# One-hot rows for eight tokens by three 16-bit VectorE instructions, gate matmuls in groups of sixteen, in an encoder trunk with retrieval layers

## The reference

```python
def peer_ffn(x, norm_g, w_query, sub_keys, u_table, v_table):
    h = rmsnorm(x, norm_g).reshape(T, D)
    q = (h @ w_query).reshape(T, PEER_HEADS, 2, PEER_DHALF)
    s = jnp.einsum('thpd,hpnd->thpn', q, sub_keys)
    vals, idx = lax.top_k(s, 16)
    cand = vals[:, :, 0, :, None] + vals[:, :, 1, None, :]
    cidx = idx[:, :, 0, :, None] * 128 + idx[:, :, 1, None, :]
    top_s, pos = lax.top_k(cand.reshape(T, 8, 256), 16)
    experts = jnp.take_along_axis(cidx.reshape(T, 8, 256), pos, axis=-1)
    gates = jax.nn.softmax(top_s, axis=-1)
    act = gelu(einsum('td,ted->te', h, u_table[experts]))      # 128 experts of 16384 for each token
    return einsum('te,ted->td', gates * act, v_table[experts])
```

## Time and profile before

| | |
|---|---|
| median of 3 runs | 1985.92 us (1985.66 to 1987.83) |
| span of the profiled execution | 1985.3 us, 42726 instructions |
| TensorE matmul busy | 1949.5 us (98%) |
| TensorE weight load busy | 1712.1 us (86%) |
| VectorE busy | 1559.7 us (79%) |
| ScalarE busy | 1313.5 us (66%) |
| mean granted TensorE clock | 0.994 of full speed |
| DMA | 326.15 MB, 164 GB/s over the span |

### The profile page before, as it was taken

How to read it: one execution, slowest core, us unless ns; L and a number is a source line. 1 busy time by engine, 2 the same in 40 slices (tenths; PEclk the granted TensorE clock), 3 DMA queues, 4 the chain that set the end, 5 groups by cost and what they waited for, 6 DMA issues and landing times.

```text
span 1985.3 us, 42726 instructions
## 1 busy us (share of the span) xinstructions
PE 1949.5 (98%) x13762; PEld 1712.1 (86%) x13762; DVE 1559.7 (79%) x3516; ACT 1313.5 (66%) x2799; POOL 17.5 (1%) x21
## 2 busy tenths in 40 slices
PE   8999999999999999999998999999999999999998
PEld 7778999999998777788876699999999977777887
DVE  5455699988889999755578657998888899996555
ACT  5454444589998999644465644445899989995444
POOL 0000000000000000000000000100000000000000
PEclk9999999999999999999999999999999999999999
DMA  6504455544444455555544144555444445545554
GB/s 217 170 12 163 146 182 188 180 162 167 163 165 161 167 169 169 181 188 184 189 172 135 54 160 149 170 184 197 157 160 168 161 163 165 168 169 188 184 188 158
DMA packets 89490, 326.15 MB, mean 164 GB/s; under 512 B 10064, under 2 KB 10192, under 8 KB 89040
## 3 DMA queue, kind: packets, MB, share of 16 engines
q1 hardware_dynamic: 88848, 323.00, 48.7%
q10 hardware_dynamic: 576, 2.33, 0.3%
HBM read 324.24 MB, written 1.05 MB: 164 GB/s over the span
## 4 chain that ended last, share of the span: by engine, by line
PE 93%; DVE 4%; ACT 2%; issue 1%; DMA 0%; DVEq 0%; ACTq 0%
PE ps L1467 37%; PE ps L1259 15%; PE ps L1260 14%; PE ps L1261 14%; PE ps L1418 3%; PE ps L1283 2%; PE ps L1284 2%; PE ps L1285 2%; DVE wl L748 1%; PE ps L1356 1%; PE ps L1399 1%; PE ps L1230 1%; PE ps L1350 0%; PE ps L1519 0%; ACT big L437 0%
## 5 line engine op out<-in xcount | busy, mean ns | idle before, releaser
L748 DVE TENSOR_TENSOR wl<-raw,wh 128x1024 fp32r<-128x1024 f32 x612 | 748.6, 1229 | 190.3 <-ACT wh L419 182.5
L419 ACT ACTIVATE wh<-raw 128x1024 fp32r<-128x1024 f32 x612 | 642.2, 1051 | 230.2 <-PE ps L1261 96.8
L1259 PE MATMUL ps<-hTh,wh 128*128 128x256 f32 x2376 | 684.0, 288 | 2.0 <-DVE hTl L758 2.0
L1260 PE MATMUL ps<-hTl,wh 128*128 128x256 f32 x2376 | 672.4, 283 | 0.0
L1261 PE MATMUL ps<-hTh,wl 128*128 128x256 f32 x2376 | 672.1, 283 | 0.0
L1259 PEld LDWEIGHTS ps<-hTh,wh 128*128 128x128 f32 x2376 | 455.4, 192 | 2.9 <-issue 1.8
L1260 PEld LDWEIGHTS ps<-hTl,wh 128*128 128x128 f32 x2376 | 455.5, 192 | 0.0
L1261 PEld LDWEIGHTS ps<-hTh,wl 128*128 128x128 f32 x2376 | 455.2, 192 | 0.0
L1467 PE MATMUL ps<-wh,stage_h 128*128 128x512 f32 x1024 | 333.5, 406 | 0.0
L1467 PE MATMUL ps<-wh,stage_l 128*128 128x512 f32 x1024 | 323.0, 396 | 0.0
L1467 PE MATMUL ps<-wl,stage_h 128*128 128x512 f32 x1024 | 322.8, 396 | 0.0
(11 more groups left out here) (204 smaller groups left out, 1373.5 us busy)
## 6 DMA issues: line engine op xcount, KB each, us to landing
raw<-stream SPq DMA_DIRECT2D x612, 512.0 KB, 3.3
big<-keys ACTq DMA_DIRECT2D x2, 1024.0 KB, 7.8
x<-x_in SPq DMA_DIRECT2D x1, 1024.0 KB, 5.7
out<-x SPq DMA_DIRECT2D x4, 256.0 KB, 2.2
sm<-small ACTq DMA_DIRECT2D x1, 228.5 KB, 6.0
pos_i<-positions ACTq DMA_DIRECT2D x1, 1.0 KB, 6.8
```

The lines of the kernel that those rows point to most:

```text
L419: act.activation(wh[:, r, :], raw[:, r, :], ACT.Copy).then_inc(high_ready, 1)
L748: dve.tensor_tensor(wl[:, r, :], raw[:, r, :], wh[:, r, :].bitcast(F32), ALU.subtract).then_inc(split_ready, 1)
L1259: pe.matmul(out, w_h[:, kd, :], hTh[:, kd, :], start=(kd == 0), stop=False)
L1260: pe.matmul(out, w_h[:, kd, :], hTl[:, kd, :], start=False, stop=False)
```

## The change

`GROUP` goes from 4 to 8, so a half of j has 32 groups and the two layers 128. A group's sixteen matmuls of 64 columns stand behind every second up unit (odd ones) and ahead of every second down unit (even ones). Every PSUM bank of a group is now filled: 8 tokens by 64.

The rows are made by VectorE alone, in three instructions for eight tokens, whose operands are all 16-bit: `same_j` (is j equal, 8 by 64), `hots_i` (is i equal, 8 by 128), and `hots_j` = `same_j` times the gate parts (8 by 2 by 64). The slot numbers and gates are stored twice in a row (`slot_d`, `gate_d`), so that each operand's innermost run is two neighbouring elements. ScalarE makes no rows. The last instruction waits for the first by a new semaphore `same_ready`. `slotT`, its clearing, and the fp32 `iota` are gone; `iota_h` has 128 columns. `stage_h` and `stage_l` lie in the first half of `hTh` and `hTl`, which are not read in the down projection.

```diff
-GROUP = 4
+GROUP = 8
+TURN_GROUPS = TURN // 2
...
-        slotT = sb("slotT", [P, 4, S])
+        slot_d = sb("slot_d", [P, 2, S, 2], F16)
+        gate_d = sb("gate_d", [P, S, 2, 2], F16)
+        same_j = sb("same_j", [P, 2, GROUP, HALF], F16)
...
-        stage_h = sb("stage_h", [P, 2, 2 * S], F32R)
-        stage_l = sb("stage_l", [P, 2, 2 * S], F32R)
+        stage_h = hTh[:, 0:4, :].rearrange("p (b j) t -> p b (j t)", b=2)
+        stage_l = hTl[:, 0:4, :].rearrange("p (b j) t -> p b (j t)", b=2)
...
-                def rows_of_i(half, group, turn):
...
-                def next_rows(half, r, turn0, turn):
...
-            dve.memset(slotT[:], 0.0)
...
-                dve.tensor_copy(slotT[:, 0:2, 0:S], ps[:, 4, :].rearrange("p (a t) -> p a t", a=2)
-                                ).then_inc(hi_bank_free, 1)
+                dve.tensor_copy(slot_d[:], ps[:, 4, :].rearrange("p (a t) -> p a t", a=2).unsqueeze(3)
+                                .to_broadcast([P, 2, S, 2])).then_inc(hi_bank_free, 1)
                 chain(dve.tensor_scalar(gate_h[:], ps[:, 5, 0:S], GATE_SCALE, None, ALU.mult))
-                dve.tensor_copy(slotT[:, 2, 0:S], gate_h[:])
-                dve.scalar_tensor_tensor(out=slotT[:, 3, 0:S], in0=ps[:, 5, 0:S], scalar=GATE_SCALE, in1=gate_h[:],
-                                         op0=ALU.mult, op1=ALU.subtract).then_inc(hi_bank_free, 1)
+                gate_2 = gate_h[:].unsqueeze(2).to_broadcast([P, S, 2])
+                dve.tensor_copy(gate_d[:, :, 0, :], gate_2)
+                dve.scalar_tensor_tensor(out=gate_d[:, :, 1, :],
+                                         in0=ps[:, 5, 0:S].unsqueeze(2).to_broadcast([P, S, 2]), scalar=GATE_SCALE,
+                                         in1=gate_2, op0=ALU.mult, op1=ALU.subtract).then_inc(hi_bank_free, 1)
...
-                    for k in range(GROUP):
-                        col = offset(turn, TURN * GROUP, group * GROUP + k)
-                        if k < ACT_TOKEN:
-                            dve.tensor_scalar(hots_i[:, group % 2, k, :], iota[:], slotT[:, 0, bass.ds(col, 1)],
-                                              None, ALU.is_equal)
-                        i = dve.scalar_tensor_tensor(
-                            out=hots_j[:, group % 2, k],
...
+                    dve.tensor_tensor(same_j[:, b].rearrange("p k (j two) -> p k j two", two=2),
+                                      pairs[:, half * HALF // 2:(half + 1) * HALF // 2].unsqueeze(1)
+                                      .to_broadcast([P, GROUP, HALF // 2, 2]),
+                                      slot_d[:, 1, tokens, :].unsqueeze(2).to_broadcast([P, GROUP, HALF // 2, 2]),
+                                      ALU.is_equal).then_inc(same_ready, 1)
+                    dve.tensor_tensor(hots_i[:, b].rearrange("p k (i two) -> p k i two", two=2),
+                                      pairs.unsqueeze(1).to_broadcast([P, GROUP, P // 2, 2]),
+                                      slot_d[:, 0, tokens, :].unsqueeze(2).to_broadcast([P, GROUP, P // 2, 2]),
+                                      ALU.is_equal)
+                    dve.wait_ge(same_ready, made)
+                    dve.tensor_tensor(hots_j[:, b].rearrange("p k a (j two) -> p k a j two", two=2),
+                                      same_j[:, b].rearrange("p k (j two) -> p k j two", two=2).unsqueeze(2)
+                                      .to_broadcast([P, GROUP, 2, HALF // 2, 2]),
+                                      gate_d[:, tokens, :, :].unsqueeze(3).to_broadcast([P, GROUP, 2, HALF // 2, 2]),
+                                      ALU.mult).then_inc(hot_ready, 1)
...
                     pe.wait_ge(hot_ready, w + (HOT * l + GROUPS * half + 1))
-                    pe.wait_ge(hot_ready_a, w + (HOT * l + GROUPS * half + 1))
...
                         up(r, turn)
-                        weights(0, r, HALF // TURN, turn)
+                        if r % 2 == 1:
+                            weights(0, r // 2 - HALF // 2, turn)
...
-                            if half == 0:
-                                weights(1, r, 0, turn)
+                            if half == 0 and r % 2 == 0:
+                                weights(1, r // 2, turn)
```

More of the change, by code:

```diff
@@ L591, in ffn @@
                 preload(ACT.Gelu)
[L592 to L602, removed]
+                up(EXP_AT, U_E - TURN)
                 for u in range(U_E - TURN, U_E):
@@ L1012, in one_hots @@
[L1012 to L1018, removed]
+                    b = group % 2
+                    tokens = bass.ds(offset(turn, TURN_GROUPS * GROUP, group * GROUP), GROUP)
+                    made = offset(turn, TURN_GROUPS, HOT * l + GROUPS * half + group + 1)
@@ new lines, in one_hots @@
+                    pairs = iota_h[:].rearrange("p (j two) -> p j two", two=2)
+                    dve.tensor_tensor(same_j[:, b].rearrange("p k (j two) -> p k j two", two=2),
[3 more added lines that the diff above has]
+                                      ALU.is_equal).then_inc(same_ready, 1)
@@ L1019, in weigh @@
+                def weigh(half, group, turn):
+                    dve.wait_ge(w_mm, offset(turn, TURN_GROUPS, GROUPS * (2 * l + half) + group + 1))
+                    g = G[:, half * HALF:(half + 1) * HALF,
+                          bass.ds(offset(turn, TURN_GROUPS * GROUP, group * GROUP), GROUP)]
                     dve.scalar_tensor_tensor(
-                        out=g, in0=ps[:, 4 + r % 4, 0:GROUP * HALF].rearrange("p (t j) -> p j t", t=GROUP),
+                        out=g, in0=ps[:, 4 + group % 4, :].rearrange("p (t j) -> p j t", t=GROUP),
@@ L1021, in weigh, with next_hots @@
                         scalar=1.0 / GATE_SCALE, in1=g, op0=ALU.mult, op1=ALU.mult).then_inc(hi_bank_free, 1)
-                def next_hots(half, r, turn0, turn):
-                    group = r - TURN * turn0
+                def next_hots(half, group, turn):
                     if turn is not None or group < GROUPS - 2:
@@ L1076, in ffn @@
                             put(u // 2 + 1, None)
-                        if half == 0:
-                            weigh(1, u, 0, None)
-                            next_hots(1, u, 0, None)
+                        if half == 0 and u % 2 == 0:
+                            weigh(1, u // 2, None)
+                            next_hots(1, u // 2, None)
                         if u != HALF - 1:
@@ L1417, in weights @@
                         for part in range(2):
-                            i = pe.matmul(ps[:, 4 + r % 4, k * HALF:(k + 1) * HALF], hots_i[:, r % 2, k, :],
-                                          hots_j[:, r % 2, k, part, :], start=(part == 0), stop=(part == 1))
+                            i = pe.matmul(ps[:, 4 + group % 4, k * HALF:(k + 1) * HALF], hots_i[:, group % 2, k, :],
+                                          hots_j[:, group % 2, k, part, :], start=(part == 0), stop=(part == 1))
                     i.then_inc(w_mm, 1)
```

69 lines of the change are left out of this document (18 added, 51 removed).

## The result

The changed kernel takes 1959.99 us, the median of four runs (1959.12 to 1960.14), beside 1986.76 us for the kernel before in the same comparison: a ratio of 0.9868, 95% interval 0.9856 to 0.988. The forecast was 1974.7 us, 1971 to 1980. The sign was right; the gain, 26.8 us, is more than twice the 12.1 us (1986.8 - 1974.7) that remain of the forecast against this median, and outside the range.

The account below looks back on a forecast made before the run. The prediction took TensorE as the bound, busy 98% of the span. From 1985.3 us it took 10.9 for merged gate groups and 0.3 at the start, giving 1974.1 of span; the runs' median lies 0.6 above: 1974.7 us, range 1971 to 1980.

Parts of the forecast that it names:

- What bounds the kernel: All four long stages: TensorE is the bound, its matmul side busy 160.00 of 160.00 or 170.00 of 170.00 us.
- The switch: TensorE's return from 16-bit gates to fp32 costs 0.08 us per switch; 128 merged groups save 0.085 each, 10.9 us.
- The down term: Gated down half: eight gates cost 0.319 us by window counts; merging two groups saves 0.085 us, as in the up half.
- So does every other matmul of the long stages: TensorE's long stages: all matmuls besides the gates stay as they are, so no gain or loss was counted.
- sharing `hTh` adds no wait: Stage tiles in `hTh`: the first `put` already waits for the last `weigh`, behind the last up unit; no cost.
- The start: Before the long stages: clearing `slotT` goes, 0.91 us of VectorE; gain between 0 and 0.37 us, taken as 0.3.
- VectorE at two elements for each step: New row instructions take 0.417 and 0.685 us, 1.79 for eight tokens; a down pair's 5.04 us hides within 6.14.
- The slower rival: Gated down half: VectorE's rows run one element per step or lose overlap; 15 to 31 us more, 1989 to 2005; chance 0.06.
- ScalarE's relief: Gated down half: ScalarE loses two instructions per token, busy falling from 91% to about 45%; worth 0, not the bound.
- The feed: Rival: sixteen-gate bursts outrun TensorE's sequencer, the last eight at 0.10 us each; 72 us more, 2046 us; chance 0.02.

Follow-up runs that it names:

- a_split: The changed kernel with each group's sixteen gate matmuls given in two bursts of eight again, one at each unit; 1969.6 us, ratio 0.9916.
- a_off32: The changed kernel with `stage_h` and `stage_l` moved 32 bytes further into `hTh` and `hTl`; 1973.15 us, ratio 0.9933.
- a_off256: The changed kernel with `stage_h` and `stage_l` moved 256 bytes further into `hTh` and `hTl`; 1956.11 us, ratio 0.9844.
- a_pad896: The changed kernel with 896 unused bytes ahead of `raw`, shifting every tile behind and no distance between them; 1955.69 us, ratio 0.9849.
- a_wh32: The changed kernel with `wh` and `wl` moved 32 bytes further and the tiles behind them 128; 1979.85 us, ratio 0.9966.
- b_alias: The kernel before with only `stage_h` and `stage_l` laid into the first half of `hTh` and `hTl`; 1973.49 us, ratio 0.9932.

## Why the prediction was right and where it failed

**What bounds the kernel**: right. TensorE full in all four stages before and after.

**The switch**: right, and confirmed by a_split. Its size was a little low. Forecast 0.085 us for a merged pair everywhere, 10.9 us. Measured: 0.080 in the up stage (6.387 to 6.307), and in the down stage 0.113 with the old distance (6.266 before, 6.153 in a_off32) and 0.140 with the new one (6.185 in a_split, 6.045 after); 12.4 or 14.1 us in all. The down term came out small in part because I took a group's 0.319 us there from counts in windows; by starts it is 3.133 - 2.800 = 0.333 in the kernel before. A window whose edge falls in a burst counts up to eight too many; starts of two like events are the better ruler.

**"So does every other matmul of the long stages"**, with "sharing `hTh` adds no wait": this is the step that failed. It is true that no wait was added, but I costed the moved tiles by their waits alone and took the duration of 3072 matmuls as given. They became faster: 128 plain down units by 0.080 us, 10.2, and 64 gated pairs by 0.108 (a_off32 to after), 6.9; 17.1 us that were in no term and no rival (17.0 and 17.5 by the medians of a_off256 and a_pad896, 13.2 by after's own). a_off32 is the change without this effect, and it takes 1973.15 us where 1974.7 were forecast. The sum for what I had seen was close, if with the down term too small; the range had no room for a mechanism left out.

The trace of before held a hint: its matmuls of 512 columns in the token projections have `hTh` and `hTl` as stationary operand, the same form as in the down projection, and start 0.227 us apart there, not 0.233. Timeline of the kernel before:

```profile
50.72 0.39 PE L1283 MATMUL ps<-wh,hTh 128*128 128x512 f32 x1
50.95 0.39 PE L1284 MATMUL ps<-wl,hTh 128*128 128x512 f32 x1
51.18 0.39 PE L1285 MATMUL ps<-wh,hTl 128*128 128x512 f32 x1
51.40 0.39 PE L1283 MATMUL ps<-wh,hTh 128*128 128x512 f32 x1
```

Two groups of one form and one clock with different steps ask for a reason; I compared neither. a_wh32 shows the reason above: there these matmuls start 0.234 us apart as well.

**The start**: nothing measurable, 0.3 forecast; the stretch ahead of the long stages moves by more than that with the clock from one execution to the next.

**VectorE at two elements for each step**: right to 2 ns, and hidden: 143.66 of 170 us in the gated down half (85%, forecast 82%). The Trainium skill (Vector Engine (DVE) Microarchitecture Reference, section 5.1) allows that mode for rows of two 16-bit elements, and the trace agrees with 415 and 683 ns. The slower rival did not come about.

**ScalarE's relief**: worth nothing, as said; 74.06 of 170 us busy.

**The feed**: sixteen gates run at even steps behind the first; behind thirty-two the return is about 0.03 us late in the up stage, far from the 72 us of the rival.

**Open**: behind a burst the next ten down matmuls run slower in the kernels with the good distance (704.67 to 705.60, 0.93 us for four, where 0.907 is usual) and not in the others, 0.04 us in all for a burst. With a burst at each down unit b_alias pays it twice in a pair, so it gains less than expected, and merging saves more where the distance is good (0.140) than where it isn't (0.113). Why these steps are slower is not known. What in the hardware makes the distance count wasn't found, nor whether 256 bytes is the whole rule: of multiples of 256 only 0 and 256 past 512 were tried, and 128 and 384 past 512, alike by that rule, differ a little (0.2333 and 0.2324 us a matmul).

## What to carry to other kernels

When TensorE is the bound, a change of where an operand lies can be a change of its work: compare the start-to-start steps of like matmuls across stages, and price moved tiles as well as moved waits. Give short matmuls of another type in few long bursts, since here each return cost about 0.08 us; the second doubling, to thirty-two, brought half as much in the up stage (0.04 us instead of 0.08 for each burst saved). And take an edit's parts apart on the chip even when the total is better than forecast; here about half of the gain (13.2 of 26.8 us by the medians, 17.1 of 29.4 by the stages) came from the part that was only meant to save space.

## What the runs showed of the hardware that was not expected

fp32 matmuls with 128 by 128 stationary and 512 moving columns start 0.227 us apart on average where the two operands begin a multiple of 256 bytes apart in a partition, and 0.232 to 0.234 where they are 32, 64, 96 or 128 bytes off. With 256 moving columns the step stays at 0.120 us in the one run that tried it, a_wh32 at 96 bytes off (1336 matmuls in 240 to 400 us, as in before and after). The Trainium skill (SBUF — State Buffer, "SBUF: two separate sides") says that PE never waits on another engine's port. The traces agree: a gated up pair takes 6.387 us both in b_alias, where ScalarE is busy 154.69 of 170 us, and in a_split, where it is busy 69.50. The Trainium skill (TensorE: Matmul & The Clock Gate, Part 2) has the stationary and the moving operand on two independent read ports, so that loading the next stationary operand takes no bandwidth from the running matmul. Neither lets one expect the 3% found here between layouts; the measurement decides. A return from 16-bit matmuls of 64 columns to the fp32 stream costs 0.08 us whether 8 or 16 stood in front of it, and about 0.12 behind 32 in the up stage.
